# An mLSTM and stick-breaking decoder kernel: transposes planned with a later landing, and half of the second layer's input weights cast while they are loaded

## What is computed

```python
# layer A: mLSTM, 8 heads, query/key width 128, value width 256
u = x @ w_in; qk, v, o, z, gates = split(u)
q, k = split(silu(causal_conv4(qk)))
h = mlstm(q, k, v, gates)            # recurrence over chunks, state C (128 x 256) and n
h = sigmoid(o) * (headnorm(h) * head_g) * silu(z)
x = LN(alpha * x + h @ w_out)
# layer B: stick-breaking attention, 16 heads of width 128
k, v = split(x @ kv_w); q, z = split(x @ b_w_in)
s = q @ k.T * 128 ** -0.5             # strictly causal
a = sigmoid(s) * prod_{between}(1 - sigmoid(s))
x = LN(alpha * x + ((a @ v) * silu(z)) @ b_w_out)
```

## Time and profile before

| what | value |
|---|---|
| time, median of 3 runs | 2759.37 us (2734.62 to 2774.48) |
| the profiled execution | 2728.98 us, its slowest core's span 2727.7 us (core 2) |
| spans of the 8 cores | 2678.0 to 2727.7 us |
| granted TensorE clock, mean of a core | 0.958 to 0.967 |
| PE busy | 2475.2 us (91%) |
| DVE, POOL, ACT busy | 1733.5 us (64%), 1290.4 us (47%), 1034.4 us (38%) |
| packets of POOL's DMA queue | 142.69 MB, 29.7% of the time of 16 DMA engines |
| packets of SP's DMA queue | 214.06 MB, 37.3% |
| end of the first head's products, of layer A's heads | 98 us, 1072 us |
| layer A's output projection | 1091 to 1314 us |
| layer B's heads, its output projection | 1314 to 2470 us, 2470 to 2728 us |

### The profile page before, as it was taken

The page is one execution under the profiler, slowest core; times in us unless marked ns, Lnnn a source line. Parts: engine busy times, 40 slices in busy tenths (PEclk is TensorE's granted clock), DMA queues, the critical chain, the costliest instruction groups (busy, mean ns, idle before and its releaser), DMA issues.

```text
span 2727.7 us, 37420 instructions; the slowest of 8 cores (2678.0 to 2727.7 us)
## 1 busy us (share of the span) xinstructions
PE 2475.2 (91%) x11811; PEld 1136.8 (42%) x11811; DVE 1733.5 (64%) x2859; ACT 1034.4 (38%) x1877; POOL 1290.4 (47%) x1163
## 2 busy tenths in 40 slices
PE   7788988878889886999989999999999999998997
PEld 3343433333344333444434444444444444443443
DVE  2776666656567666566456666666666666656665
ACT  2444443435354444132333444444344344431111
POOL 2554654545455544243345555455555455533433
PEclk9798989988889898999989999999999999999998
DMA  9476877877878776687445656666765555667851
GB/s 155 79 106 101 128 94 114 95 100 100 109 95 127 114 122 187 228 238 210 120 100 119 124 117 120 119 128 121 121 126 103 112 108 111 136 149 188 257 207 78
DMA packets 520191, 359.14 MB, mean 132 GB/s; under 512 B 454208, under 2 KB 487104, under 8 KB 506560
## 3 DMA queue, kind: packets, MB, share of 16 engines
q1 hardware_dynamic: 492688, 214.06, 37.3%
q0 software_dynamic: 27312, 142.69, 29.7%
HBM read 289.60 MB, written 100.66 MB: 143 GB/s over the span
## 4 chain that ended last, share of the span: by engine, by line
PE 59%; DMA 16%; DVE 10%; SPq 6%; issue 4%; POOL 3%; ACT 2%; another core or an unknown queue 0%; DVEq 0%; ACTq 0%; POOLq 0%
PE PSA L1098 23%; PE PSA L937 15%; PE PSA L604 11%; DMA REGH<-REGX 9%; DVE REGW L1206 6%; SPq L160 5%; PE PSA L1264 4%; PE PSA L1179 3%; DMA REGX<-REGW 2%; PE PSA L552 1%; DMA REGW<-REGW 1%; DMA REGX<-x_t 1%; POOL REGW L1232 1%; DMA REGW<-a_wu 1%; DMA mida<-REGW 1%
## 5 line engine op out<-in xcount | busy, mean ns | idle before, releaser
L1098 PE MATMUL PSA<-REGH,REGX 128*128 128x512 bf16 x4096 | 976.3, 380 | 5.9 <-DVE REGW L1105 5.9
L1206 DVE TENSOR_TENSOR_SCAN REGW<-PSA,REGW 128x512 f32<-128x512 f32 (+3 forms) x640 | 684.9, 1091 | 299.4 <-ACT PSA L1184 231.1
L1232 POOL TENSOR_TENSOR REGW<-REGW 128x1024 bf16<-128x1024 f32 (+7 forms) x384 | 527.2, 1391 | 358.2 <-DMA REGX<-REGW 185.2
L1098 PEld LDWEIGHTS PSA<-REGH,REGX 128*128 128x128 bf16 x4096 | 397.5, 98 | 462.2 <-issue 10.4
L1184 ACT ACTIVATE PSA<-PSA 128x512 f32<-128x512 f32 (+3 forms) x640 | 326.8, 519 | 304.2 <-PE PSA L1179 298.8
L604 PE MATMUL PSA<-REGH,REGW 128*128 128x512 bf16 x1680 | 424.7, 394 | 0.0
L604 PE MATMUL PSA<-REGX,REGW 128*128 128x512 bf16 x1680 | 414.8, 388 | 4.1 <-DVE REGW L650 3.0
L604 PEld LDWEIGHTS PSA<-REGH,REGW 128*128 128x128 bf16 x1680 | 167.6, 101 | 183.6 <-issue 22.7
L1110 ACT CAST REGW<-PSA 128x512 bf16<-128x512 f32 x192 | 112.7, 587 | 346.5 <-PE PSA L1098 344.1
L604 PEld LDWEIGHTS PSA<-REGX,REGW 128*128 128x128 bf16 x1680 | 164.8, 100 | 184.6 <-issue 15.8
L937 PE MATMUL PSA<-REGX,REGW 128*128 128x512 bf16 x1024 | 223.5, 382 | 18.6 <-DMA REGW<-mida 18.6
(11 more groups left out here) (142 smaller groups left out, 2518.6 us busy)
## 6 DMA issues: line engine op xcount, KB each, us to landing
REGW<-a_wu POOLq DMA_DIRECT2D x64, 512.0 KB, 9.1
REGX<-wb POOLq DMA_DIRECT2D x64, 512.0 KB, 4.6
y<-REGW SPq DMA_DIRECT2D x26, 1024.0 KB, 4.2
wb<-kv_w POOLq DMA_DIRECT2D x64, 256.0 KB, 9.1
wb<-b_w_in POOLq DMA_DIRECT2D x64, 256.0 KB, 8.5
REGW<-y SPq DMA_DIRECT2D x14, 1024.0 KB, 6.8
REGW<-x SPq DMA_DIRECT2D x13, 1024.0 KB, 6.8
wao<-a_w_out POOLq DMA_DIRECT2D x32, 256.0 KB, 6.3
```

The lines of the kernel that those rows point to most:

```text
L1098: yield Op("pe", lambda c=c: P_.matmul(PS[bank], lhsT=WS[i % 4][:, c, :], rhs=X1[tb][:, c, :], start=(c == 0), stop=(c == KC - 1)), R=[f"W ...
L1206: yield Op("dve", lambda: V.tensor_tensor_scan(out=RR[slot][:, lo:hi][:, ::-1], data0=PS[bank][:, 0:w][:, ::-1], data1=mk[:, ::-1], initia ...
L1232: yield Op("pool", lambda: G.tensor_tensor(out=AA[:, (pos + b0) * 128:(pos + b1) * 128], in0=RR[slot][:, lo + 1:hi + 1], in1=RR[slot][:, l ...
```

## The change

The planner gets a parameter for how long after the DMA clock a transfer counts as landed. It stays at 1.2 us, but the transposes to `KN`, `VN` and `HT` of layer A are planned with 14 us (`LATE`). This changes no instruction, only the order in which the engines run them. The transposes of layer B keep 1.2 us.

Only heads 0 to 7 (`PRE`) of `kv_w` and `b_w_in` are now copied to bf16 in DRAM, with 64 DMAs in place of 128, and a cast is issued every 4.0 slots in place of 2.45. The units of heads 8 to 15 are loaded into the ring straight from the float32 weights, with the cast in that load, and without a wait for the copies. Such a load counts 4.0 us in the plan and not 1.5.

```diff
+LATE = 14.0
+PRE = 8
-    def dma(self, q, slot, out, in_, R=(), W=(), A=(), cost=4.0, **kw):
+    def dma(self, q, slot, out, in_, R=(), W=(), A=(), cost=4.0, lat=1.2, **kw):
...
-        self._time(self.tdma + 1.2, R, W)
+        self._time(self.tdma + lat, R, W)
...
-            for h in range(NH_B):
+            for h in range(PRE):
...
-                yield lambda: at("slot") >= 10 + 2.45 * i
+                yield lambda: at("slot") >= 10 + 4.0 * i
...
-                                      in_=KTa[:, tb * 512:(tb + 1) * 512], transpose=True))
+                                      in_=KTa[:, tb * 512:(tb + 1) * 512], transpose=True, lat=LATE))
...
-                                      in_=VTa[:, tb % 2, u, :], transpose=True))
+                                      in_=VTa[:, tb % 2, u, :], transpose=True, lat=LATE))
...
-                         dma=dict(slot=f"ht{i % NHT}", out=HT[i % NHT], in_=HB[i % 4], transpose=True))
+                         dma=dict(slot=f"ht{i % NHT}", out=HT[i % NHT], in_=HB[i % 4], transpose=True, lat=LATE))
...
-                yield Op("pool", None, R=["CAST"], W=[f"WB{i % 4}"], cost=1.5,
-                         dma=dict(slot=f"wb{i % 4}", out=WSA[:, i % 4, :], in_=wb16[i]))
+                src, r = (wb16[i], ["CAST"]) if i < 4 * PRE else \
+                    ((b_w_in if i % 2 else kv_w)[(i % 4 // 2) * 16 + i // 4].rearrange("p c n -> p (c n)"), [])
+                yield Op("pool", None, R=r, W=[f"WB{i % 4}"], cost=1.5 if r else 4.0,
+                         dma=dict(slot=f"wb{i % 4}", out=WSA[:, i % 4, :], in_=src))
```

More of the change, by code:

```diff
@@ L455, in casts @@
         def casts():
-            halves = lambda o, i, n: [(o[k * n:(k + 1) * n], i[k * n:(k + 1) * n]) for k in range(2)]
             ca, cb, co = [], [], []
@@ L459, in casts @@
                 for p in range(0, 128, 32):
-                    ca += halves(wao16[nb, p:p + 32], a_w_out[nb, p:p + 32], 16)
-                    co += halves(wo16[nb, p:p + 32], b_w_out[nb, p:p + 32], 16)
-            for h in range(NH_B):
+                    for k in range(p, p + 32, 16):
+                        ca.append((wao16[nb, k:k + 16], a_w_out[nb, k:k + 16]))
+                        co.append((wo16[nb, k:k + 16], b_w_out[nb, k:k + 16]))
+            for h in range(PRE):
                 for i, (w, u) in enumerate(((kv_w, h), (b_w_in, h), (kv_w, 16 + h), (b_w_in, 16 + h))):
-                    cb += halves(wb16[4 * h + i].rearrange("p (c n) -> p c n", c=KC), w[u], 64)
+                    o = wb16[4 * h + i].rearrange("p (c n) -> p c n", c=KC)
+                    for k in range(0, 128, 64):
+                        cb.append((o[k:k + 64], w[u][k:k + 64]))
             for i, (out, in_) in enumerate(ca + cb):
-                yield lambda: at("slot") >= 10 + 2.45 * i
+                yield lambda: at("slot") >= 10 + 4.0 * i
                 yield Op("pool", None, cost=1.5, dma=dict(slot="casta" if i < len(ca) else "cast", out=out, in_=in_))
```

## The result

The changed kernel takes 2585.65 us in the median of 3 runs (2585.38 to 2724.17). Forecast were 2628 us, with a range from 2585 to 2710, so the measured median lies just inside its low end. Beside three other kernels in a later session, the ratio was 0.947 (0.936 to 0.959). The two sessions agree within their intervals, so the change is worth 5 to 6%.

The account below looks back on a forecast made before the run. Layer A's heads were taken as bound by PE plus an order reading key tiles too early. Terms -114 - 24 + 3 + 5 = -130 us gave 2599 us, ratio 0.952, carried over to 2628 us; range 2585 to 2710 us.

Parts of the forecast that it names:

- The bound: Layer A's heads: PE plus an order that reads key tiles too early; in layer B's heads only PE work.
- The stops: Layer A's heads: reading transposed tiles later removes PE's waits tied to ACT's L779, -114 us (-122 to -90).
- The clock: Layer A's heads: fewer stops of PE bring a higher granted clock, -24 us.
- the proportional bound of 33 us: Layer A's heads: of 41 us lost to the lower clock, 33 return if they go in proportion with the stops.
- The end of layer A: Before the output projection: three uncovered steps and the load of mida cost 22 us where 18.6, +3 us (-8 to +14).
- The float32 loads: Layer B: 32 units loaded from float32, landing in 8.8 us, PE not waiting for weights; +5 us, 0 to 18.
- The upper bound of 3.8 us of DMA time for a load: Layer B: each of 32 float32 loads adds at most 3.8 us for the DMA engines, 122 us in 580.
- The rival on layer B: Layer B: float32 loads make its transposes late and PE stands each time, +46 us, 2806 us; chance 5%.
- The sum: Whole kernel: all terms together -130 us on 2728.98 us, 2599 us for an execution like the profiled one.
- the 1.1% between profile and median: Whole kernel: the profiled execution lay 1.1% under the median 2759.37 us; carrying the ratio over gave 2628 us.
- the first rival: Layer A's heads: waits move to the head norm's four HB buffers, only -17 us, 2742 us; chance 12%.
- The sign I named: Layer A's heads: PE waiting at L794 on L853 without ACT waiting at L783 would show the forecast wrong.

Follow-up runs that it names:

- pre0: The changed kernel (14 us planned) without copies of kv_w and b_w_in, all 64 units of layer B loaded from float32: ratio 0.943, later 0.947, against the kernel before.
- k_only: The kernel before with 14 us planned for the transposes to KN alone, casts unchanged: ratio 0.978, 61 us faster.
- late_only: The kernel before with 14 us planned for all three transposes of layer A, casts unchanged: ratio 0.958, 113 us faster.
- pre0_late8: The changed kernel without copies of kv_w and b_w_in and with 8 us planned in place of 14: ratio 0.954 against the kernel before.
- pre0_early: The kernel before without copies of kv_w and b_w_in, all transposes planned with 1.2 us: ratio 0.959, 113 us faster.
- pre_only: The kernel before with 64 casts in place of 128, heads 8 to 15 loaded from float32, transposes planned with 1.2 us: ratio 0.973, 75 us faster.

## Why the prediction was right, and where it was not

*The bound.* The rows were read rightly: the time was to be had in layer A's heads alone. They ended at 933 us, where the prediction had 98 + 835.

*The stops.* Forecast -114 us. PE's idle time in layer A's heads went from 152 to 835 - 791.6 = 43 us, so -109 us. ACT's wait at L783 was to be under 20 us, and is 17.8, as one stop and not as several short ones. In the median core the idle time fell by 98 us, from 133 to 35.

*The clock.* Forecast -24 us between bounds of 14 and 33, by stops. PE's busy time fell by 30 us at a granted clock of 0.98: the proportional bound of 33 us was nearer than the middle. That is 1.1% of the span of 2728 us, and the 41 us that the prediction worked out are 1.5%. The Trainium skill, "TensorE: Matmul & The Clock Gate", section "Part 1: The HAM clock gate", has under 1% of a typical kernel's span, and says it of the warm-up at a start. This kernel paid after many stops, so the figure was no bound for it, and the prediction should not have used it as one.

*The end of layer A.* Forecast +3 us, measured 11.7 - 19.0 = -7 us (from the starts of the last product and the first matmul of the output projection, 933.0 to 944.7 and 1071.8 to 1090.8). This term was wrong in its size and its sign, though inside its bounds of -8 to +14. I had added the load of `mida` to the three steps, but it was issued at 922.4 us and was there when the steps, 11 us as forecast, were over. PE's wait there was to be near 22 us.

*The float32 loads.* Forecast +5 us for layer B, measured 0.2 us to layer B's output projection (1378.0 against 1377.8) and 2 us more behind it. A load was to land in about 9 us, and landed in 5.7 to 6.3. The upper bound of 3.8 us of DMA time for a load was far off: POOL's queue took 23.3% of 577 us in place of 16.3% of 580, 40 us more for 29 loads, so 1.4 us more for each. In layer A the price was nearer: the 64 copies that went took 53.5% of 974 less 46.2% of 835, some 135 us, with them, where 122 were forecast. The rival on layer B, by which its transposes fall behind, is refuted by pre0, with twice as many such loads.

*The sum.* -130 us forecast, -143.7 us measured between the two slowest cores; over the 8 cores the median span fell by 128 us. For an execution like the profiled one the forecast was 2599 us, and 2585.65 was measured. The median of runs fell by more, 174 us, because the 1.1% between profile and median that the prediction carried over was a matter of those three runs: before took 2727.5 and 2729.9 us in two later sessions. That carrying put the forecast at 2628 us, and that the result still lies in the range, 0.65 us above its low end, is in part luck.

*The cause as I told it failed in part.* Two sentences don't hold. The first gave the lighter traffic "no gain for it, since the time is hidden already once the waits are". In the changed kernel that is nearly so, but the traffic is a large part of why the transposes were late: with the old plan, dropping half of the copies brings 75 us and dropping all of them 113. The second took the key tiles' readers for the whole loss. Most waits of PE above 5 us did lead back to L779, and against the rival it was said that none like it shows that isn't behind L779. One was overlooked, in the kernel before:

```profile
184.93 0.29 DVE L865 TENSOR_TENSOR REGW<-REGW 128x256 bf16<-128x256 bf16 x1 [6.59 <-DMA REGW<-REGW]
```

```profile
187.47 0.37 PE L806 MATMUL PSA<-REGW 128*128 128x257 bf16 x1 [7.34 <-DVE REGW L846]
```

DVE stood for a transpose to `HT`, and PE stood behind it, while ACT was not at L779. k_only shows that the readers of `HT` and the writers of `HB` were badly placed as well: with the keys alone, 52 of 113 us stay away, and the first rival, stops at the head norm's buffers, comes true. That these stops were hidden behind ACT's in the kernel before is the likely reading; that k_only's own order made some of them is not excluded. With all the casts in flight, late_only still has three such stops of ACT (19.8 us); the changed kernel, with `HT` planned late and half of the copies gone, has 0.4 us. The forecast came out by that, and not by its argument.

*What would show it wrong.* The sign I named, PE waiting at L794 on L853 without ACT waiting at L783, is there in the changed kernel, but small: 11.6 of the 20.2 us, as 8.6 stand behind ACT's one stop at L783. What is left of the loss, 43 us of idle time, is in many short waits, of which these are the largest group.

## What to carry to other kernels

Where engines run in a planned order, a landing that is planned too early costs each engine behind it, and the fix is one number in the plan. Try it on every transfer of the kind: here the key tiles alone brought 61 us and keys and head outputs together 108, while the v tiles added nothing that could be told. Ask also why the transfer is late: here, dropping all copies of weights that nobody needed yet brought as much as the plan did, and casting them in the load that uses them cost layer B a few us at most, since the ring of buffers covered it. Planning later than needed costs at the end of a stage, where the work pushed back has no cover (a gap of 23.0 us in place of 11.7 with 20 us in the plan), and planning too early costs there as well, where it puts the next stage's first load late (22.8 us in pre0_late8).

## What the hardware showed

The issue of a transpose takes SP 1.2 us in the median (1.5 for those to `VN` before), but not always. SP's instructions in layer A's heads, as duration in ns min/median/max, before and in pre0:

```profile
L160 SPq DMA_TRANSPOSE REGW<-REGW x124: 1167/1179/12816, 113.0 to 1050.8; - x124
...
L160 SPq DMA_TRANSPOSE REGH<-REGX x30: 1188/1194/7462, 133.3 to 1049.4; - x30
```

```profile
L162 SPq DMA_TRANSPOSE REGW<-REGW x124: 1167/1174/3207, 115.1 to 922.8; - x124
...
L162 SPq DMA_TRANSPOSE REGW<-REGH x58: 1188/1198/3281, 110.3 to 875.3; - x58
L162 SPq DMA_TRANSPOSE REGH<-REGX x30: 1188/1189/2371, 133.9 to 899.1; - x30
```

With the copies of the second layer's weights in flight an issue of a transpose took up to 12.8 us before and in the changed kernel, and in k_only up to 13.9 us; without them, 3.3 us at most in pre0 and 3.6 us in pre0_early. The longest issue doesn't follow the number of copies: pre_only, with as many as the changed kernel, has 5.1 us. All that stands behind a long issue on SP is late by as much, and no DMA row shows that, as the time to landing counts from the issue. The Trainium skill has, in "DMA: Bandwidth & Descriptors", section "SWDGE vs HWDGE vs iDMA", that a DMA engine takes turns between the queues of the two kinds. The later landings under the casts agree with it (transposes to `VN`, 9.0 us with all the copies and 2.4 us with none); whether the long issues come from the same is not shown.
